# Two-block transformer on one Trainium2 core: the routing pipeline ahead of the experts, its instructions in another order

## The chip, the cores and the metric

The kernel runs on one core of one Trainium2 chip. The metric is the device time of one execution in microseconds, and the number given is the median of several runs. The core's engines are named as in the profile: PE is TensorE, DVE is VectorE, ACT is ScalarE, POOL is GpSimd, SP is SyncE, which here only issues transfers.

## What is computed

Two model blocks follow each other on an input of 512 rows by 1024. The first has two layers (pooling, retention and memory attention; then a sparse attention with memory attention). The second has a Fourier mix, a state-space mix and a mixture of experts. The change lies where the mixture of experts is prepared:

```python
x = x + merged @ w_out[i]
hn = _rmsnorm(x, ffn_norm_g[i])
x = x + _hier_moe(hn, router_group_w[i], ...)
...
x_pad = jnp.zeros((rows, d), h.dtype).at[dest].set(ht[tok_s])
a = jax.nn.silu(xb @ w_gate[e]) * (xb @ w_up[e])
return a @ w_down[e]
```

The router picks one of 8 groups for each row, and in it two of 8 experts, so 1,024 assignments go to 64 experts. Each expert has three float32 matrices (gate, up, down) of 1024 by 512 or 512 by 1024, 2,048 KB each, 192 in all. The output is the sum of each row's two weighted expert results, added to x and normalized.

## The kernel before

The program is a list of stages. The last two are `mix_out` and `moe`, and they share one block, with no barrier between them: each engine goes from its part of one to its part of the other when it gets there. Every engine's order is written out by hand, and engines meet at semaphores.

`mix_out` projects the merged mix (`project(n, m)`: column half n, row tile m of 4), adds it to `h` on DVE (`add`), normalizes each row tile (`norm` on DVE, the square sums and roots on ACT), turns h for the router (`turn` on PE, copies `take_hT` on DVE and line 2588 on ACT), computes the router's logits (`logits` on PE), chooses experts (`choose` on DVE), and ranks each row within its expert (`ranks` on PE, `rank` on DVE, which also makes the 0/1 matrix `picks0`). `hn` is split into a high and a low part: ACT rounds the high part (line 2590, semaphore `hn_high`), and POOL subtracts it from hn (line 2471, semaphore `hn_low`). `gather(m)` on PE multiplies both parts with `picks0` and so collects, in 4 PSUM banks, the rows of the first four experts. The banks are cleared beforehand by matmuls with zeros (line 2521). DVE copies the banks to `xT` (line 2681, semaphore `first_taken`), and counts per expert are made by PE (line 2568) and copied by DVE (line 2688).

`moe` then goes over 64 experts, e = 0 to 63. For each PE computes gate and up (`hidden`, line 2835, 64 instructions of weights and matmuls in two passes), gathers the rows of expert e + 4 (line 2815), turns the activated product, and after each pair of experts computes both results (`result`, line 2850). `place` (line 2827) makes row addresses once in 4 experts.

The 192 expert matrices are parts n = 0 to 191, six for each pair of experts: gate, up, gate, up, down, down. They land in 8 homes, part n in home n % 8. The first 8 are loaded by SP in `mix_out`. The homes of parts 5, 6 and 7 lie over memory that `mix_out` still uses: `h`, `hn`, and the block of `hT`, `picks0` and `zeros`. SP's queue waits for each in order:

```python
            sp.wait_ge(added, 2 * NT)
            sp.dma_start(k.x3_dram.rearrange("(m p) n -> p m n", p=P), h).then_inc(k.x3_stored, 16)
...
            sp.wait_ge(k.x3_stored, 16)
            load_expert_part(k, sp, 5)
            sp.wait_ge(hn_low, NT)
            load_expert_part(k, sp, 6)
            sp.wait_ge(lg_mm, NT)
            sp.wait_ge(gathered0, KD // 2)
            load_expert_part(k, sp, 7)
```

Parts 3 and 4 wait for `chunk_used`, the ends of the projection's two halves. In `moe` a part is loaded as soon as its home is free: part 8 when gate of expert 0 is done, part 9 when up of expert 0 is done, and so on, four of each six by SP and two (gate and up of one expert) by POOL after a pair's results.

Of the kernel before, what the change touches and what calls it, by code (L numbers as in the profile page):

```python
# [2348 lines left out]
def part_at(i, r):  # L2349

    return 6 * (i // 2) + (2 * (i % 2) + r if r < 2 else 4 + i % 2)
# [32 lines left out]
def mix_out(k):  # L2384
# [40 lines left out]
         "first_gathered", "first_taken"))  # L2425
    k.first_gathered, k.first_taken, k.counted = gathered0, taken0, c_mm
    first_banks = (0, 1, 6, 7)

    with k.block() as block:
# [35 lines left out]
        @block.gpsimd  # L2465
        def _(pool):
            pool.memset(ones, 1.0).then_inc(done, 1)
            pool.memset(k.zeros[0:1].bitcast(F32), 0.0).then_inc(zeros_set, 1)
            for m in range(NT):
                pool.wait_ge(hn_high, m + 1)  # L2470
                pool.tensor_tensor(k.hn_parts[:, 1, m, :, :], by_part[:, m, :, :],
                                   k.hn_parts[:, 0, m, :, :].bitcast(F32), ALU.subtract).then_inc(hn_low, 1)

        @block.tensor
        def _(pe):
# [8 lines left out]
            def turn(m):  # L2484
                pe.wait_ge(added, NT + m + 1)
                if m:
                    pe.wait_ge(hT_act, m)
                    pe.wait_ge(hT_dve, m)
                for j in range(2):
                    for kk in range(4):  # L2490
                        t = pe.transpose(k.ps[:, 2 + j, kk * P:(kk + 1) * P],  # L2491
                                         h[:, m, (4 * j + kk) * P:(4 * j + kk + 1) * P], k.ident)
                    t.then_inc(h_T, 1)
# [22 lines left out]

            def clear_first_banks():

                pe.wait_ge(zeros_set, 1)
                for b in first_banks:  # L2520
                    pe.matmul(k.ps[:, b, :], k.zeros[0:1, 0:P], k.zeros[0:1], start=True, stop=False)
# [30 lines left out]
            turn(2)  # L2552
            ranks(0)
            project(1, 3, range(KD // 2, KD))
            logits(2)
            turn(3)
            ranks(1)
            clear_first_banks()
            gather(0)
            logits(3)  # L2560
            ranks(2)
# [3 lines left out]
            gather(3)  # L2565
            pe.wait_ge(lg_in, NT)
            for m in range(NT):
                mm = pe.matmul(k.ps[:, 4, 0:NE], ones, M[:, m, :], start=m == 0, stop=m == NT - 1)
            mm.then_inc(c_mm, 1)

        @block.scalar
        def _(act):
# [4 lines left out]
            for m in range(NT):  # L2577
# [8 lines left out]
                if m >= 2:  # L2586
                    act.wait_ge(lg_mm, m - 1)
                act.copy(hT[:, m % 2, 4:8, :], k.ps[:, 3, :].rearrange("p (k s) -> p k s", k=4)).then_inc(hT_act, 1)
                act.wait_ge(gained, m + 1)
# [7 lines left out]
        def _(dve):  # L2597
# [17 lines left out]
            def norm(m):  # L2615
                dve.wait_ge(rooted, m + 1)
                k.link(dve, dve.reciprocal(rs[:, m:m + 1], sd[:, m:m + 1]))
                dve.scalar_tensor_tensor(out=hn[:, m, :], in0=h[:, m, :], scalar=rs[:, m:m + 1], in1=gain,
                                         op0=ALU.mult, op1=ALU.mult).then_inc(gained, 1)

            def choose(m):
# [39 lines left out]
            take_hT(0)  # L2661
            norm(0)
            add(1, 2)
            take_hT(1)
            choose(0)
            norm(1)
            norm(2)
            take_hT(2)
            choose(1)
            rank(0)  # L2670
            add(1, 3)
            take_hT(3)
            norm(3)
            choose(2)
            rank(1)
            rank(2)
            choose(3)
            rank(3)
            for piece in range(KD // 2):
                dve.wait_ge(gathered0, piece + 1)  # L2680
# [5 lines left out]
            k.link(dve, dve.tensor_reduce(sm[:, 4, :], eg, AX_X, ALU.add))  # L2686
            dve.wait_ge(c_mm, 1)
            k.link(dve, dve.tensor_copy(k.route.cnt, k.ps[:, 4, 0:NE]))

# [65 lines left out]
def moe(k):  # L2755

    nc, ps = k.nc, k.ps
    xT = k.xT
    t = k.misc
# [15 lines left out]
    with k.block() as block:  # L2775
# [27 lines left out]
        def _(pe):  # L2803
# [27 lines left out]
            def hidden(e, bank, w, done):  # L2831
                x = xT[:, e // FOUR % 2, :, SLOTS * (e % FOUR):SLOTS * (e % FOUR + 1)]
                for kk in range(KD):
                    for h in range(2):
                        mm = pe.matmul(ps[SLOTS * h:SLOTS * (h + 1), bank, 0:256], x[:, kk, :],  # L2835
                                       w[:, kk, 256 * h:256 * (h + 1)], start=kk == 0, stop=kk == KD - 1)
                mm.then_inc(done, 1)

            def result(pair):
                pe.wait_ge(aT_ready, 2 * pair + 2)  # L2840
                if pair:
# [13 lines left out]
            for e in range(NE):  # L2855
                if e < FOUR:
                    pe.wait_ge(k.first_taken, KD // 2)
                else:
                    pe.wait_ge(x_ready, 4 * (e // FOUR))
# [8 lines left out]
                wait_expert_part(k, pe, part_at(e, 1))  # L2868
                hidden(e, UP, expert_view(k, part_at(e, 1)), up_done)
                if e % FOUR == 0:  # L2870
                    place(e // FOUR)
# [31 lines left out]
        def _(dve):  # L2903
# [29 lines left out]
            for e in range(NE):  # L2933
                dve.wait_ge(silu_done, e + 1)
                dve.wait_ge(up_done, e + 1)
                if e >= 2:
                    dve.wait_ge(turned, e - 1)
                dve.tensor_tensor(a[:, e % 2, :], sg[:, e % 2, :], ps[:, UP, 0:256], ALU.mult).then_inc(a_ready, 1)  # L2938
                if e + FOUR < NE:
                    take(e + 4)  # L2940
# [340 lines left out]
```

## Time and profile before

| | us |
|---|---|
| median of 3 runs | 2478.43 (2476.04 to 2483.17) |
| profiled execution, its own time | 2479.41 |
| its span | 2477.6 |
| PE busy | 2250.2 (91%) |
| DVE busy | 793.8 (32%) |
| ACT busy | 471.3 (19%) |
| POOL busy | 251.4 (10%) |
| TensorE's granted clock, mean share | 0.967 |

The span is what the engines' records cover. The profiled execution took 1.8 us more than its span and 1.0 us more than the median. Busy shares are means over a dozen stages with different limits, so what a change in one stage is worth has to be read in that stage. `mix_out` runs from about 1406 to 1499 us of the span, `moe` from there to the end.

### The profile page before, as it was taken

The page shows a single profiled execution, that of the slowest core. Times are in us where ns is not written, and L with a number is a line of the kernel's source. Part 1 is how long each engine was busy: PE and PEld are TensorE (multiplying, and loading weights), DVE is VectorE, ACT ScalarE, POOL GpSimd, SP SyncE. Part 2 cuts the span into 40 slices and gives each one's busy share as a digit, 9 for nine tenths or more (in the row PEclk, how much of TensorE's full clock was granted, in tenths as well). Part 3 has the DMA queues.
Part 4 walks back from the last instruction along what each step waited for, and adds up shares of the span by engine and source line. Part 5 has one row for each costly group of instructions (what it writes and reads, how often), then busy time and mean ns, then how long its engine had stood idle before and what let it go on. Part 6 is the DMA issues. An engine that isn't in the chain of part 4 may idle for free. (4 is left out here: it accounts for less than half of the span.)

```text
span 2477.6 us, 32053 instructions
## 1 busy us (share of the span) xinstructions
PE 2250.2 (91%) x13664; PEld 1643.0 (66%) x13664; DVE 793.8 (32%) x1645; ACT 471.3 (19%) x834; POOL 251.4 (10%) x232
## 2 busy tenths in 40 slices
PE   8899978999999998899988999989998998889984
PEld 5788857888888677778874456555555555555552
DVE  6453246233322777444252242111111111111102
ACT  3222213131132544242211030000000000000001
POOL 0620000011000000650000010000000000000000
PEclk9999999999998999999999999999999999999997
DMA  7443212344331000435163449999999999999996
GB/s 220 154 136 119 69 46 86 109 160 145 97 119 34 10 22 14 171 128 174 56 122 120 148 173 383 426 425 425 426 425 425 424 425 423 421 421 426 424 420 241
DMA packets 130835, 569.16 MB, mean 230 GB/s; under 512 B 30563, under 2 KB 44503, under 8 KB 96855
## 3 DMA queue, kind: packets, MB, share of 16 engines
q1 hardware_dynamic: 110308, 409.47, 43.6%
q0 software_dynamic: 19232, 153.41, 15.3%
q10 hardware_dynamic: 1152, 4.19, 0.5%
q8 instruction: 111, 1.82, 0.3%
q14 instruction: 32, 0.26, 0.0%
HBM read 543.63 MB, written 35.80 MB: 234 GB/s over the span
## 5 line engine op out<-in xcount | busy, mean ns | idle before, releaser
L476 PE MATMUL ps<-w_parts,u_parts 128*128 128x512 f32 (+3 forms) x2016 | 426.2, 372 | 13.5 <-DVE u_parts L656 6.8
L476 PEld LDWEIGHTS ps<-w_parts,u_parts 128*128 128x128 f32 x2016 | 363.2, 189 | 71.7 <-DVE u_parts L656 8.0
L2835 PE MATMUL ps<-mem,mem_u 128*64 128x256 f32 x3072 | 348.3, 382 | 6.0 <-DVE mem_u L2919 3.8
L2835 PEld LDWEIGHTS ps<-mem,mem_u 128*64 128x64 f32 x3072 | 225.7, 137 | 118.8 <-issue 15.5
L443 DVE TENSOR_TENSOR w_parts<-w_raw,w_parts 128x2048 fp32r<-128x2048 f32 (+3 forms) x76 | 170.3, 2241 | 395.1 <-ACT w_parts L438 395.1
L2938 DVE TENSOR_TENSOR mem_c<-mem_c,ps 128x256 f32<-128x256 f32 x64 | 26.9, 421 | 712.7 <-issue 586.5
L2850 PE MATMUL ps<-mem,mem_c 128*64 128x512 f32 x768 | 191.5, 656 | 60.2 <-DMA mem<-in_expert_w_down 59.6
L438 ACT CAST w_parts<-w_raw 128x2048 fp32r<-128x2048 f32 (+3 forms) x76 | 134.9, 1776 | 486.0 <-PE ps L476 194.2
L2850 PEld LDWEIGHTS ps<-mem,mem_c 128*64 128x64 f32 x768 | 66.6, 150 | 174.1 <-issue 173.0
L474 PE MATMUL ps<-u_parts,w_parts 128*128 128x512 f32 x768 | 176.8, 390 | 0.0
L1442 PE MATMUL ps<-w_parts,u_parts 128*128 128x512 f32 x768 | 174.9, 390 | 0.0
L474 PEld LDWEIGHTS ps<-u_parts,w_parts 128*128 128x128 f32 x768 | 143.6, 188 | 31.2 <-issue 1.7
L1442 PEld LDWEIGHTS ps<-w_parts,u_parts 128*128 128x128 f32 x768 | 144.3, 188 | 29.9
L2896 ACT ACTIVATE mem_c<-ps 128x256 f32<-128x256 f32 x64 | 24.6, 385 | 571.9 <-PE ps L2835 571.9
L2815 PE MATMUL ps<-picks,hn_parts 128*128 128x256 f32 x960 | 130.6, 289 | 0.0
L2815 PEld LDWEIGHTS ps<-picks,hn_parts 128*128 128x128 f32 x960 | 118.4, 191 | 17.3 <-issue 17.3
L2835 PE MATMUL ps<-mem_u 128*64 128x256 f32 x1024 | 115.4, 381 | 4.1 <-DVE mem_u L2919 3.8
L2835 PEld LDWEIGHTS ps<-mem_u 128*64 128x64 f32 x1024 | 74.6, 137 | 41.7 <-DVE mem_u L2919 5.1
L2890 ACT COPY mem_u<-ps 128x512 f32<-128x512 f32 x64 | 34.4, 589 | 319.4 <-PE ps L2850 319.4
L1804 PEld LDWEIGHTS ps<-mem_u 128*128 128x128 f32 x480 | 59.0, 191 | 30.8 <-ACT mem_u L1859 24.2
L2365 POOL DMA_DIRECT2D mem<-in_expert_w_gate x23 | 12.9, 560 | 649.6 <-PE ps L2850 649.6
L1804 PE MATMUL ps<-mem_u 128*128 128x128 f32 x480 | 63.5, 279 | 16.2 <-ACT mem_u L1859 16.0
(390 smaller groups left out, 2359.3 us busy)
## 6 DMA issues: line engine op xcount, KB each, us to landing
mem<-in_expert_w_down SPq DMA_DIRECT2D x48, 2048.0 KB, 33.1
mem<-in_expert_w_gate SPq DMA_DIRECT2D x25, 2048.0 KB, 36.7
mem<-in_expert_w_up SPq DMA_DIRECT2D x25, 2048.0 KB, 27.7
mem<-in_expert_w_gate POOLq DMA_DIRECT2D x23, 2048.0 KB, 13.9
mem<-in_expert_w_up POOLq DMA_DIRECT2D x23, 2048.0 KB, 23.2
mem_u<-in_expert_w_down SPq DMA_DIRECT2D x16, 2048.0 KB, 34.6
w_raw<-in_od_w_in SPq DMA_DIRECT2D x18, 1024.0 KB, 5.0
mem_u<-in_expert_w_gate SPq DMA_DIRECT2D x9, 2048.0 KB, 36.7
```

Source lines behind the costliest of these rows:

```text
L438: act.copy(self.part(n, 0), self.raw(n)).then_inc(self.high, 1)
L443: dve.tensor_tensor(self.part(n, 1), self.raw(n), self.part(n, 0).bitcast(F32), ALU.subtract).then_inc(self.low, 1)
L474: mm = pe.matmul(out, w[x][:, kk, g.t * P:(g.t + 1) * P], u[:, y, ku, :], start=first, stop=last)
L476: mm = pe.matmul(out, u[:, x, ku, g.t * P:(g.t + 1) * P], w[y][:, kk, :], start=first, stop=last)
L1442: mm = pe.matmul(k.ps[:, g.bank, :], parts[g.part // 2][:, x, ky, g.t * P:(g.t + 1) * P], w[z][:, kk, :], start=g.part == 0 and kk == 0 an ...
L1804: mm = pe.matmul(o[:, 128 * i:128 * i + 128], pT[v % 2][:, 512 * i + kt * P:512 * i + kt * P + P], vv[:, kt, g * DH:(g + 1) * DH], start=k ...
L2815: mm = pe.matmul(o, k.hn_parts[:, part, m, 2 * r + j, :], k.picks[:, q % 2, m, :, :], start=m + part == 0, stop=m == NT - 1 and part == 1)
L2835: mm = pe.matmul(ps[SLOTS * h:SLOTS * (h + 1), bank, 0:256], x[:, kk, :], w[:, kk, 256 * h:256 * (h + 1)], start=kk == 0, stop=kk == KD - 1)
L2850: mm = pe.matmul(ps[SLOTS * i:SLOTS * (i + 1), ROWS + c, :], aT[:, i, j, SLOTS * h:SLOTS * (h + 1)], w[i][:, h, j, 512 * c:512 * (c + 1)], ...
L2890: act.copy(yn[:, pair % STORES, 512 * c:512 * (c + 1)], ps[:, ROWS + c, :]).then_inc(rows_ready, 1)
L2896: act.activation(sg[:, e % 2, :], ps[:, GATE, 0:256], ACT.Silu).then_inc(silu_done, 1)
L2938: dve.tensor_tensor(a[:, e % 2, :], sg[:, e % 2, :], ps[:, UP, 0:256], ALU.mult).then_inc(a_ready, 1)
```

## The change

No arithmetic is changed. (1) The subtraction that makes the low part goes from POOL to DVE, as `low(m)`; POOL has no compute in the stage after two memsets. (2) On DVE the last addition `add(1, 3)` still follows `rank(0)`, but norm(1) and norm(2), the low parts and the `take_hT` copies stand elsewhere; both last choices precede the ranks 2 and 3, and `low(3)` is last before the copies of the gathered banks. (3) On PE three banks are cleared inside the last projection, `ranks(1)` comes before `logits(2)`, and `logits(3)` comes ahead of `gather(0)`. For this the fourth turned tile uses bank 7 for its second half, and the gathers use bank 3 in place of 7. (4) In `moe` the gate of expert 0 waits for `first_taken` piece by piece, and the counts (four matmuls) and their copy stand behind the up of expert 0.

```diff
--- before.py
+++ after.py
@@ -2423,8 +2423,10 @@
...
          "first_gathered", "first_taken"))
-    k.first_gathered, k.first_taken, k.counted = gathered0, taken0, c_mm
-    first_banks = (0, 1, 6, 7)
+    k.first_taken, k.count_done = taken0, c_mm
+    k.ones, k.M = ones, M
+    first_banks = (0, 1, 6, 3)
+    turn_banks = [(2, 3)] * (NT - 1) + [(2, 7)]
 
...
@@ -2466,10 +2468,6 @@
...
             pool.memset(k.zeros[0:1].bitcast(F32), 0.0).then_inc(zeros_set, 1)
-            for m in range(NT):
-                pool.wait_ge(hn_high, m + 1)
-                pool.tensor_tensor(k.hn_parts[:, 1, m, :, :], by_part[:, m, :, :],
-                                   k.hn_parts[:, 0, m, :, :].bitcast(F32), ALU.subtract).then_inc(hn_low, 1)
 
...
@@ -2488,7 +2486,7 @@
...
                     for kk in range(4):
-                        t = pe.transpose(k.ps[:, 2 + j, kk * P:(kk + 1) * P],
+                        t = pe.transpose(k.ps[:, turn_banks[m][j], kk * P:(kk + 1) * P],
                                          h[:, m, (4 * j + kk) * P:(4 * j + kk + 1) * P], k.ident)
...
@@ -2514,10 +2512,9 @@
...
 
-            def clear_first_banks():
-
-                pe.wait_ge(zeros_set, 1)
-                for b in first_banks:
+            def clear(banks):
+
+                for b in banks:
                     pe.matmul(k.ps[:, b, :], k.zeros[0:1, 0:P], k.zeros[0:1], start=True, stop=False)
...
@@ -2551,22 +2548,20 @@
...
             ranks(0)
+            pe.wait_ge(zeros_set, 1)
+            clear(first_banks[0:3])
             project(1, 3, range(KD // 2, KD))
+            ranks(1)
             logits(2)
             turn(3)
-            ranks(1)
-            clear_first_banks()
+            clear(first_banks[3:4])
+            logits(3)
             gather(0)
-            logits(3)
             ranks(2)
...
             gather(3)
-            pe.wait_ge(lg_in, NT)
-            for m in range(NT):
-                mm = pe.matmul(k.ps[:, 4, 0:NE], ones, M[:, m, :], start=m == 0, stop=m == NT - 1)
-            mm.then_inc(c_mm, 1)
 
...
@@ -2585,7 +2580,8 @@
...
                     act.wait_ge(lg_mm, m - 1)
-                act.copy(hT[:, m % 2, 4:8, :], k.ps[:, 3, :].rearrange("p (k s) -> p k s", k=4)).then_inc(hT_act, 1)
+                act.copy(hT[:, m % 2, 4:8, :], k.ps[:, turn_banks[m][1], :].rearrange("p (k s) -> p k s", k=4)
+                         ).then_inc(hT_act, 1)
                 act.wait_ge(gained, m + 1)
...
@@ -2617,6 +2613,11 @@
...
                                          op0=ALU.mult, op1=ALU.mult).then_inc(gained, 1)
+
+            def low(m):
+                dve.wait_ge(hn_high, m + 1)
+                dve.tensor_tensor(k.hn_parts[:, 1, m, :, :], by_part[:, m, :, :],
+                                  k.hn_parts[:, 0, m, :, :].bitcast(F32), ALU.subtract).then_inc(hn_low, 1)
 
...
@@ -2660,22 +2661,26 @@
...
             norm(0)
+            norm(1)
+            low(0)
             add(1, 2)
+            choose(0)
             take_hT(1)
-            choose(0)
-            norm(1)
             norm(2)
+            low(1)
             take_hT(2)
...
             add(1, 3)
+            rank(1)
+            low(2)
             take_hT(3)
...
             choose(2)
-            rank(1)
+            choose(3)
             rank(2)
-            choose(3)
             rank(3)
+            low(3)
             for piece in range(KD // 2):
...
@@ -2684,8 +2689,6 @@
...
             k.link(dve, dve.tensor_reduce(sm[:, 4, :], eg, AX_X, ALU.add))
-            dve.wait_ge(c_mm, 1)
-            k.link(dve, dve.tensor_copy(k.route.cnt, k.ps[:, 4, 0:NE]))
 
...
@@ -2755,7 +2758,7 @@
...
     nc, ps = k.nc, k.ps
-    xT = k.xT
+    xT, count_out = k.xT, k.sem("moe_count_copied")
     t = k.misc
...
@@ -2831,12 +2834,22 @@
...
                 for kk in range(KD):
+                    if done is gate_done and e == 0:
+                        pe.wait_ge(k.first_taken, kk // 2 + 1)
                     for h in range(2):
...
 
+            def count():
+
+                for m in range(NT):
+                    mm = pe.matmul(ps[:, ROWS, 0:NE], k.ones, k.M[:, m, :], start=m == 0, stop=m == NT - 1)
+                mm.then_inc(k.count_done, 1)
+
             def result(pair):
+                if pair == 0:
+                    pe.wait_ge(count_out, 1)
                 pe.wait_ge(aT_ready, 2 * pair + 2)
...
@@ -2853,9 +2866,7 @@
...
             for e in range(NE):
-                if e < FOUR:
-                    pe.wait_ge(k.first_taken, KD // 2)
-                else:
+                if e >= FOUR:
                     pe.wait_ge(x_ready, 4 * (e // FOUR))
...
@@ -2867,6 +2878,8 @@
...
                 hidden(e, UP, expert_view(k, part_at(e, 1)), up_done)
+                if e == 0:
+                    count()
                 if e % FOUR == 0:
...
@@ -2936,6 +2949,9 @@
...
                 dve.tensor_tensor(a[:, e % 2, :], sg[:, e % 2, :], ps[:, UP, 0:256], ALU.mult).then_inc(a_ready, 1)
+                if e == 0:
+                    dve.wait_ge(k.count_done, 1)
+                    dve.tensor_copy(k.route.cnt, ps[:, ROWS, 0:NE]).then_inc(count_out, 1)
                 if e + FOUR < NE:
...
```

The order on PE at the end of `mix_out`, from the last half of the turned tile 1 to the first gathers. L2479 and L2477 are the projection, L2503 and L2501 logits, L2491 and L2489 turns, L2514 to L2515 and L2512 to L2513 ranks, L2521 and L2518 clears, L2529 and L2526 gathers. Before:

```order
L2491 MATMUL ps<-mem_c,mem 128x128 x8
L2515 MATMUL ps<-mem_u 128x64
L2479 MATMUL ps<-mem,mem_u 128x512 x4
L2503 MATMUL ps<-mem_u,mem 128x72 x8
L2491 MATMUL ps<-mem_c,mem 128x128 x8
L2514 MATMUL ps<-mem_u 128x64
L2515 MATMUL ps<-mem_u 128x64
L2521 MATMUL ps<-zeros 128x512 x4
L2529 MATMUL ps<-picks_55,hn_parts 128x256 x16
L2503 MATMUL ps<-mem_u,mem 128x72 x8
```

and now:

```order
L2489 MATMUL ps<-mem_c,mem 128x128 x8
L2513 MATMUL ps<-mem_u 128x64
L2518 MATMUL ps<-zeros 128x512 x3
L2477 MATMUL ps<-mem,mem_u 128x512 x4
L2512 MATMUL ps<-mem_u 128x64
L2513 MATMUL ps<-mem_u 128x64
L2501 MATMUL ps<-mem_u,mem 128x72 x8
L2489 MATMUL ps<-mem_c,mem 128x128 x8
L2518 MATMUL ps<-zeros 128x512
L2501 MATMUL ps<-mem_u,mem 128x72 x8
L2526 MATMUL ps<-picks_55,hn_parts 128x256 x16
```

Three of the four clears stand ahead of the projection's last piece, and all logits are computed before the first gather.

The order on DVE around the last addition (L2607, now L2603). L2642 and L2644, now L2643 and L2645, are a `rank`; L2619 is the new `low`; L2613, now L2609, is `take_hT`; L2617 and L2618, now L2613 and L2614, are a `norm`. Before:

```order
L2642 SCALAR_TENSOR_TENSOR mem_u<-ps,mem_u 128x64
L2644 TENSOR_TENSOR picks_55<-mem_u 128x256
L2607 TENSOR_TENSOR mem<-mem,ps 128x512
L2613 COPY mem<-ps 128x512
L2617 RECIPROCAL mem_c<-mem_c 128x1
L2618 SCALAR_TENSOR_TENSOR mem<-mem,mem_c,mem_u 128x1024
```

and now:

```order
L2643 SCALAR_TENSOR_TENSOR mem_u<-ps,mem_u 128x64
L2645 TENSOR_TENSOR picks_55<-mem_u 128x256
L2603 TENSOR_TENSOR mem<-mem,ps 128x512
L2643 SCALAR_TENSOR_TENSOR mem_u<-ps,mem_u 128x64
L2645 TENSOR_TENSOR picks_55<-mem_u 128x256
L2619 TENSOR_TENSOR hn_parts<-mem,hn_parts 128x1024
L2609 COPY mem<-ps 128x512
L2613 RECIPROCAL mem_c<-mem_c 128x1
L2614 SCALAR_TENSOR_TENSOR mem<-mem,mem_c,mem_u 128x1024
```

rank(1) and low(2) now stand between the last addition and the turned tile 3.

The order on PE where `moe` begins. L2568, now L2847, are the counts, L2835, now L2840, the gate and up of expert 0. Before:

```order
L2529 MATMUL ps<-picks_55,hn_parts 128x256 x32
L2568 MATMUL ps<-mem_u 128x64 x4
L2802 UNCONDITIONAL_BRANCH
L2835 MATMUL ps<-mem_u 64x256 x32
L2827 MATMUL ps<-slot_table,picks 128x2 x8
```

and now:

```order
L2526 MATMUL ps<-picks_55,hn_parts 128x256 x32
L2805 UNCONDITIONAL_BRANCH
L2840 MATMUL ps<-mem_u 64x256 x32
L2847 MATMUL ps<-mem_u 128x64 x4
L2830 MATMUL ps<-slot_table,picks 128x2 x8
```

The counts have moved behind the first 32 matmuls of `moe`.

## Rows read from the trace of the kernel before

**Rows 1.** The page: GB/s of the DMA engines in 40 slices of the span.

```profile
GB/s 220 154 136 119 69 46 86 109 160 145 97 119 34 10 22 14 171 128 174 56 122 120 148 173 383 426 425 425 426 425 425 424 425 423 421 421 426 424 420 241
```

**Rows 2.** Windows, core 0: from:to, length, busy of five engines, PEclk, DMA share, GB/s.

```profile
1474.00:1486.00 12.00, 8.26 (x39) 7.14 (x39) 10.24 (x26) 6.10 (x7) 4.14 (x2) 0.61 0.85 337
1486.00:1489.40 3.40, 3.40 (x29) 3.40 (x27) 1.94 (x1) 0.00 (x0) 1.65 (x1) 0.86 0.32 47
1489.40:1520.00 30.60, 29.03 (x251) 23.08 (x251) 13.05 (x36) 2.38 (x5) 0.00 (x0) 1.00 0.99 388
1520.00:1550.00 30.00, 29.46 (x226) 17.79 (x224) 4.02 (x7) 2.23 (x5) 2.17 (x3) 1.00 1.00 411
1550.00:2420.00 870.00, 786.56 (x5768) 492.30 (x5764) 103.39 (x230) 53.44 (x116) 60.76 (x87) 0.97 1.01 424
```

**Rows 3.** Who waited for whom, 1600 to 2450: us in total, times, longest.

```profile
PE ps L2850 <- DMA mem<-in_expert_w_down: 59.6, 19, 5.7
```

**Rows 4.** Timeline of SyncE's queue: start us, us, engine, line, operation.

```profile
1472.18 0.38 SPq L2365 DMA_DIRECT2D mem<-in_expert_w_down  x1
1479.27 0.38 SPq L2453 DMA_DIRECT2D x<-mem  x1
1487.60 0.37 SPq L2365 DMA_DIRECT2D mem<-in_expert_w_down  x1
1488.01 0.47 SPq L2365 DMA_DIRECT2D mem<-in_expert_w_gate  x1
1498.14 0.34 SPq L2365 DMA_DIRECT2D mem<-in_expert_w_up  x1
1502.90 0.33 SPq L2365 DMA_DIRECT2D mem_u<-in_expert_w_gate  x1
```

**Rows 5.** Line 2453 alone, the store of h: its time to landing.

```profile
DMA to landing us min/median/max: 8.2/8.2/8.2
```

**Rows 6.** Timeline of VectorE, ScalarE, GpSimd; [idle before <-releaser].

```profile
1466.54 2.08 ACT L2590 CAST hn_parts<-mem 128x1024 fp32r<-128x1024 f32 x1 [3.47 <-DVE mem L2618]
...
1470.23 2.41 DVE L2618 SCALAR_TENSOR_TENSOR mem<-mem,mem_c,mem_u 128x1024 f32<-128x1024 f32 x1
...
1474.80 2.85 POOL L2471 TENSOR_TENSOR hn_parts<-mem,hn_parts 128x1024 fp32r<-128x1024 f32 x1 [3.24 <-ACT hn_parts L2590]
...
1475.06 2.73 DVE L2599 TENSOR_TENSOR mem_c<-mem_u 128x128 f32<-128x128 f32 x1
...
1478.22 0.42 DVE L2644 TENSOR_TENSOR picks<-mem_u 128x256 fp32r<-128x256 f32 x1
1478.57 0.68 DVE L2607 TENSOR_TENSOR mem<-mem,ps 128x512 f32<-128x512 f32 x1
...
1481.25 1.29 DVE L2618 SCALAR_TENSOR_TENSOR mem<-mem,mem_c,mem_u 128x1024 f32<-128x1024 f32 x1
...
1482.45 0.28 DVE L2624 SCALAR_TENSOR_TENSOR mem_u<-ps,mem_c,mem_u 128x72 f32<-128x72 f32 x1
...
1485.07 2.87 DVE L2644 TENSOR_TENSOR picks<-mem_u 128x256 fp32r<-128x256 f32 x1
```

**Rows 7.** Part 5 of the page: busy us, mean ns | idle before, releaser.

```profile
L443 DVE TENSOR_TENSOR w_parts<-w_raw,w_parts 128x2048 fp32r<-128x2048 f32 (+3 forms) x76 | 170.3, 2241 | 395.1 <-ACT w_parts L438 395.1
```

**Rows 8.** Timeline of TensorE's matmuls.

```profile
1468.50 3.65 PE L2479 MATMUL ps<-mem,mem_u 128*128 128x512 f32 x8
...
1479.30 1.97 PE L2491 MATMUL ps<-mem_c,mem 128*128 128x128 f32 x8 [3.74 <-DVE mem L2607]
...
1481.94 2.07 PE L2521 MATMUL ps<-zeros 1*128 1x512 f32 x4
...
1493.97 4.08 PE L2529 MATMUL ps<-picks,hn_parts 128*128 128x256 f32 x32
1497.89 1.00 PE L2568 MATMUL ps<-mem_u 128*128 128x64 f32 x8
1499.18 7.13 PE L2835 MATMUL ps<-mem_u 128*64 128x256 f32 x64 [0.30 <-DVE mem_u L2681]
```

## The prediction

> **What bounds the kernel now.** I read the page's GB/s over the 40 slices first [rows 1]. Up to slice 24 (1486 us) the transfers move 10 to 230 GB/s, so other things bound; from slice 26 to the one before the last they stand at 421 to 426 and never dip. That is the expert weights. The windows say the same: 424 GB/s over 870 us at a DMA share of 1.01, while TensorE is busy for 787 of these 870 [rows 2]. Then the waits: after 1600 TensorE waits 59.6 us, 19 times, for down matrices in `mem` alone [rows 3]. So from about 1550 on, the stream of weights bounds the kernel, and TensorE, although 91% busy on the page, waits for it. The chain of waits ends in these transfers too, but it does not say where their delay begins. That must be sought where the stream last had holes: at 1486 to 1489.4 (47 GB/s), 1489.4 to 1520 (388) and 1520 to 1550 (411) [rows 2].
>
> So the changed stage matters in two ways. It starts TensorE's work on the experts earlier, which is a lead that TensorE later loses again while it waits for weights. And it starts weight transfers earlier, which is kept. The end moves by what the second is worth, unless the first is less.
>
> **The change on the engines: the last addition.** Before, `add(1, 3)` starts at 1478.57, although its matmuls, begun at 1468.50 and 3.65 long, ended near 1472.2 [rows 6, 8]. DVE was late, and three of its operations were long: a normalization of 2.41 us where another takes 1.29, a comparison in choose(1) of 2.73 beside neighbours of 0.2 to 0.4, and a `picks0` of 2.87 where another takes 0.42 [rows 6]. The second began at 1475.06 and ended at 1477.79; POOL's subtraction ran from 1474.80 to 1477.65 [rows 6]. The third is as long as a subtraction. The excess is 1.1 + 2.4 + 2.45 = 6 us. With POOL's four subtractions gone I take these three back to their short form.
>
> The Trainium skill's page SBUF — State Buffer, section "SBUF: two separate sides", says that VectorE operations with two SBUF inputs and a GpSimd operation that reads SBUF exclude one another for a whole instruction. The ends at 1477.79 and 1477.65 agree with it; by that rule too the excess goes and no new one comes.
>
> DVE pays four subtractions. Their nearest row is the same operation on twice the elements, mean 2.24 us [rows 7], so I take 1.15 each, 4.6 in all. Bounds: 0.7 (the 128x512 addition's 0.68 [rows 6]) and 2.85 (POOL's).
>
> norm(1) no longer stands behind choose(0), so ACT's rounding of tile 1 need not wait the 3.47 us that it did before 1466.54 [rows 6]. ACT is then done with the root of tile 2 some 3.3 us sooner, and norm(2), which started at 1470.23 with its reciprocal just ahead, can start near 1466.9. From there DVE does norm(2) 1.5, low(1) 1.2, a copy 0.7, choose(1) 2.4 (choose(2) ran from 1482.45 to just before 1485.07 [rows 6]) and rank(0) 0.7, which is 1473.4. The projection has three clears ahead of it now. Four took 2.07 at a granted clock of half [rows 2, 8], so three take 0.8 at full clock; with 0.2 for ranks(0), its last piece ends near 1473.2. DVE and PE meet, and the addition ends at 1474.1 in place of 1479.25: **5.1 us earlier**.
>
> **From there to the first expert.** PE: ranks(1) and logits(2) to 1475.8, turn(3) to 1476.8 (1.97 at half clock [rows 8], 1.0 at full). DVE: the copy to 1477.1, norm(3) to 1478.6, choose(2) to 1481.0; its first operation, done at 1478.9, releases logits(3), which ends at 1480.8. Then gather(0) 2.0 (two gathers take 4.08 [rows 8]) to 1482.8, ranks(2) 0.75 to 1483.6 (eight matmuls of this size take 1.00 [rows 8]), gather(1) to 1485.6, ranks(3) to 1486.6; DVE's rank(3) ends at 1487.4 and low(3) at 1488.6. gather(3) ends at 1490.8, and the gate of expert 0 follows at once, since its first piece of `xT` is copied while the gather still runs. Before it started at 1499.18 [rows 8]: **8.4 us earlier**. The counts cost nothing before, as they ran at 1497.89 while DVE copied the gathered banks; now their 1.00 us stands behind expert 0's up [rows 8]. TensorE's lead from then on is 8.4 - 1.0 = 7.4 us.
>
> **What the weight stream gets.** Here SP's queue counts, with every transfer that the addition lets go [rows 4]. Part 4 was issued at 1472.18 and h's store at 1479.27; it landed 8.2 us later [rows 5], and then part 5 went out at 1487.60, part 6 at 1488.01, part 7 at 1498.14, part 8 at 1502.90. Both the first two moved in 1474 to 1486, at 337 GB/s [rows 2]. Now part 4 goes out at 1473.3 (one us later, behind the clears) and the store at 1474.2. They overlap: 4.19 MB from 1475.1 on, at 396 (337 over the DMA share of 0.85) to 424 GB/s, take 9.9 to 10.6 us, say 10.2, to 1485.3. Before, nearly all of the 4.19 MB had moved near 1485.8 (337 GB/s over 12 us is 4.04 MB) and the store landed at 1479.27 + 8.2 = 1487.5, so I add 1.7 for the landing: 1487.0. Part 5 is issued at 1487.1. Of the addition's 5.1 us only **0.5** reaches the stream, because part 4 did not come forward. Bounds: 0 and 1.5 (if the store finishes ahead of part 4).
>
> The Trainium skill's page DMA: Bandwidth & Descriptors, section "Issuing engines are not separate DMA queues", speaks against a larger gain too: transfers of all queues share the same 16 DMA engines. By that rule the sum stays as it is.
>
> Then the holes. Part 5's first bytes flow 1.8 us after its issue (1487.60 to 1489.4, with 47 GB/s until then [rows 2]), at 1488.9, and a part of 2.10 MB takes 4.95 us at 424 GB/s. Part 6 is let go by low(3) at 1488.7, part 7 at 1490.9, part 8 at 1490.8 + 3.7 = 1494.5, the 3.7 being 1502.90 - 1499.18 of before [rows 4, 8]. At each of these times there are still 3 us or more of weights ahead, and the requests that follow come 7.4 us sooner than they did. So the stream stays at 424 from 1489 on. Before it lacked (424 - 388) x 30.6 = 1.10 MB up to 1520, which is **2.6 us**, and (424 - 411) x 30 = 0.39 MB up to 1550, **0.9 us** [rows 2]. The second is doubtful, since a dip can come from the transfers' own mix. The gain is 0.5 + 2.6 to 0.5 + 3.5, and I take 3.7: it is below TensorE's lead of 7.4, so the stream decides.
>
> The profiled execution took 2479.41, of which I expect 2475.7; against the median that is 2478.43 - 3.7 = **2474.7**.
>
> **The rivals.** (A) TensorE's lead counts in full: 7.4 us, 2471.0. For it: up to 1520 TensorE is busy in 29.03 of 30.6 us [rows 2] and so sets the pace there. Against it: the 424 GB/s over 870 us [rows 2] and the wait of 59.6 us [rows 3]. 2 in 10.
>
> (B) Slower. TensorE's granted clock is 0.5 of full (1.2 GHz, not 2.4) in matmuls that follow the idle 3.74 us before 1479.30 [rows 8], and 0.61 over 1474 to 1486 [rows 2]. In the new order it still idles from 1477.0 to 1479.0, where logits(3) waits for choose(2). If the clock falls there, logits(3), gather(0), ranks(2), gather(1) and ranks(3) take twice their 7.5 us; rank(3) and low(3) stand behind them, so low(3) ends at 1496.1 and gather(3) at 1498. Part 6 was issued at 1488.01 [rows 4]; it now is out at 1496, where the weights ahead ended at 1493.9. With the counts' 1.0 us on top, expert 0's up and all behind is level with before or late. That gives 2480. It decides from the point where low(3) ends later than about 1495.8, as each us after 1492.1 opens a hole of one us, and 3.7 use up the gain. Against it: before, shorter idle pieces such as the 0.30 ahead of 1499.18 left the clock alone, though none of 2 us is shown. 1 in 10.
>
> (C) The change does nothing for the end: part 5 still waits for the store and the holes stay as the transfers' own mix. 2478.4. 1 in 10.
>
> The forecast case has 6 in 10, and by its own bounds (a gain of 2 to 6, with the scatter of a median) lies between 2472 and 2477.
>
> **How the numbers follow.** The three runs before spread over 7 us, so I count 0.3%, 7.4 us, as what can be told from no change. A centre of 2474.7 is 3.7 below, hence same. Faster by more needs case A and a bit of luck, or scatter: 1 in 10 from A (its centre is just at the bound) and 1 in 10 from the forecast case. Slower by more needs B with more than its price: 6 in 100. The rest, 74 in 100, is same. The range reaches from 2470.0, past A, to 2480.5, past B.
>
> **What the changed kernel's profile would show.** DVE's operations of 2.4 to 2.9 us are gone, and its subtractions take 1.1 to 1.3 us; h's store is issued near 1474 and part 5 near 1487; part 6 waits for DVE's last subtraction near 1488.7; expert 0's gate starts near 1491 at full clock; GB/s from 1489 to 1550 is near 424. TensorE's waits for down matrices grow by some 4 us, its lead less the stream's. I am wrong if GB/s there stays near 400, if the end moves by the whole lead, or if the clock falls again before the gathers.

## The result, and the profile after

The changed kernel's median is 2472.43 us (22 runs), the kernel's before 2477.38 (22 runs). The ratio is 0.9982, 95% interval 0.9974 to 0.999: by the ratio 4.5 us or 0.18% faster, inside what I had called the same; the two medians alone are 4.95 us apart. The forecast was 3.7 us (2474.7, counted from the 2478.43 of three runs). The span of the profiled execution went from 2477.6 to 2472.3.

The windows of the changed kernel, from:to, length, busy time of PE, PEld, DVE, ACT and POOL, granted clock, DMA share, GB/s:

```profile
1474.00:1486.00 12.00, 10.08 (x63) 9.63 (x62) 8.88 (x29) 5.37 (x6) 0.00 (x0) 0.75 0.95 344
1486.00:1489.40 3.40, 3.40 (x28) 3.40 (x27) 0.65 (x2) 0.00 (x0) 0.00 (x0) 0.89 0.24 49
1489.40:1520.00 30.60, 29.82 (x255) 22.14 (x255) 12.27 (x24) 2.76 (x6) 0.00 (x0) 1.00 1.00 417
1520.00:1550.00 30.00, 29.46 (x216) 16.96 (x214) 4.02 (x7) 1.84 (x4) 2.16 (x3) 1.00 1.01 422
1550.00:2415.00 865.00, 784.58 (x5750) 491.45 (x5746) 103.43 (x230) 53.44 (x116) 60.79 (x87) 0.96 1.01 424
```

Against [rows 2]: from 1489.4 to 1520 417 GB/s flow in place of 388, from 1520 to 1550 422 in place of 411, and after that 424 in both. The first is worth (417 - 388) x 30.6 / 424 = 2.1 us, the second 0.8. Within the first the hole lay mostly in one stretch, before and then after the change:

```profile
1500.00:1510.00 10.00, 10.00 (x92) 7.42 (x90) 4.54 (x8) 1.27 (x2) 0.00 (x0) 1.00 0.94 362
```

```profile
1500.00:1510.00 10.00, 10.00 (x90) 7.74 (x88) 1.90 (x7) 0.39 (x1) 0.00 (x0) 1.00 1.00 429
```

It stood where parts 5 and 6 were nearly through and parts 7 and 8, which the gathers and the gate of expert 0 let go, had only just gone out. Now these go out 3.5 and 4.7 us sooner (rows below) and it is gone. This is read from the order of the rows; no run moves parts 7 and 8 alone.

TensorE's longest kind of wait for weights after 1600 is as it was [rows 3]; engine, line, waited for, us in total, times, longest:

```profile
PE ps L2863 <- DMA mem<-in_expert_w_down: 58.8, 20, 5.6
```

SyncE's queue, against [rows 4]: start us, us, operation.

```profile
1473.16 0.38 SPq L2365 DMA_DIRECT2D mem<-in_expert_w_down  x1
1474.06 0.38 SPq L2455 DMA_DIRECT2D x<-mem  x1
1487.73 0.37 SPq L2365 DMA_DIRECT2D mem<-in_expert_w_down  x1
1492.36 0.34 SPq L2365 DMA_DIRECT2D mem<-in_expert_w_gate  x1
1494.65 0.34 SPq L2365 DMA_DIRECT2D mem<-in_expert_w_up  x1
1498.21 0.33 SPq L2365 DMA_DIRECT2D mem_u<-in_expert_w_gate  x1
```

The store of h goes out at 1474.06, 5.2 us sooner, and part 5 at 1487.73, not sooner at all (1487.60). Part 6 is 4.4 us later than before, part 7 3.5 and part 8 4.7 us sooner. Two rows of TensorE's timeline and then VectorE's, against [rows 6, 8]:

```profile
1479.15 2.95 PE L2501 MATMUL ps<-mem_u,mem 128*128 128x72 f32 x16 [1.92 <-DVE mem_u L2625]
1481.85 3.76 PE L2526 MATMUL ps<-picks,hn_parts 128*128 128x256 f32 x16
...
1492.38 2.18 PE L2526 MATMUL ps<-picks,hn_parts 128*128 128x256 f32 x16 [0.78 <-DVE hn_parts L2619]
```

```profile
1472.29 0.29 DVE L2595 TENSOR_TENSOR mem_c<-mem_u 128x128 f32<-128x128 f32 x1
...
1473.35 0.68 DVE L2603 TENSOR_TENSOR mem<-mem,ps 128x512 f32<-128x512 f32 x1
...
1490.28 2.05 DVE L2619 TENSOR_TENSOR hn_parts<-mem,hn_parts 128x1024 fp32r<-128x1024 f32 x1
```

The last comparison of choose(1) takes 0.29 us, not 2.73, and the last addition starts at 1473.35, not 1478.57. But the new subtraction takes 2.05 us where I had 1.15, and logits(3) and gather(0) take 2.95 and 3.76 us (1.98 and some 2.0 at full clock), since the granted clock fell to half during logits(3), which starts after 1.92 us of idle time. gather(3), which waits for the last subtraction, starts at 1492.38, and the gate of expert 0 at 1494.49.

**Positions, not times of day.** The same code ahead of the stage ends at another time in each profile. This is the projection's first matmul in a kernel whose earlier stages are unchanged; before it stood at 1410.65, in the changed kernel at 1410.60:

```profile
1404.74 5.82 PE L2480 MATMUL ps<-mem,mem_u 128*128 128x512 f32 x13 [0.83 <-ACT mem_u L2572]
```

So below every position is counted from that matmul, in us. The columns "last but one in" and "last in" are the landings of the last two of the 192 matrices, both of them down matrices: the issue plus the time to landing. The expectations call the first of them "the last weights"; the stream ends with the second. The ratio is to the kernel before, run again beside each group of kernels (its median was between 2475.5 and 2477.4). One kernel stands in the table twice, as e_contig and e_contig_timed, and its two profiles differ by 1.4 us in the one column and by 0.8 in the other, so smaller differences there say little.

| kernel | its zero | part 5 out | part 6 out | gate 0 starts | last but one in | last in | ratio, 95% interval |
| --- | --- | --- | --- | --- | --- | --- | --- |
| before | 1410.65 | 77.0 | 77.4 | 88.5 | 1024.8 | 1030.8 | 1 |
| changed | 1410.60 | 77.1 | 81.8 | 83.9 | 1021.9 | 1027.0 | 0.9982 (0.9974 to 0.999) |
| e_moe_only | 1404.74 | 77.2 | 77.6 | 87.5 | 1024.5 | 1029.4 | 0.9994 (0.9984 to 1.0003) |
| e_pool | 1407.99 | 77.1 | 77.5 | 84.6 | 1021.6 | 1026.6 | 0.9994 (0.9985 to 1.0004) |
| e_contig | 1408.51 | 77.4 | 78.4 | 80.5 | 1021.9 | 1027.1 | not timed |
| e_contig_timed | 1409.98 | 76.8 | 78.4 | 80.5 | 1020.5 | 1026.3 | 0.999 (0.998 to 0.9999) |
| e_late5 | 1406.23 | 81.8 | 82.2 | 83.9 | 1025.8 | 1031.6 | 1.0002 (0.9993 to 1.0011) |
| e_warm | 1411.29 | 77.0 | 80.1 | 82.3 | 1020.8 | 1026.6 | 0.9991 (0.9982 to 1.0) |
| e_warm_low | 1408.37 | 76.9 | 77.3 | 81.3 | 1020.4 | 1026.6 | 0.9988 (0.9979 to 0.9997) |
| e_tiles | 1405.86 | 73.8 | 80.2 | 82.3 | 1020.0 | 1025.1 | 0.9986 (0.9977 to 0.9996) |
| e_all3 | 1406.04 | 73.5 | 76.0 | 82.9 | 1019.1 | 1025.0 | 0.9974 (0.9965 to 0.9983) |
| e_tiles_low | 1407.36 | 73.1 | 75.9 | 82.8 | 1018.9 | 1024.9 | 0.9974 (0.9964 to 0.9985) |
| e_best | 1410.31 | 68.2 | 75.7 | 81.3 | 1018.2 | 1023.1 | 0.9983 (0.9974 to 0.9992) |

### The profile page after: what moved, and what is told of

The parts are those of the page before. It is cut to its first block and busy times, and to the rows that moved or that the text cites. A ratio compares the mean times of both kernels' runs of the same rounds, so it can differ in the third digit from the quotient of the medians.

```text
span 2472.3 us, 32053 instructions
## 1 busy us (share of the span) xinstructions
PE 2250.2 (91%) x13664; PEld 1643.1 (66%) x13664; DVE 797.7 (32%) x1649; ACT 471.2 (19%) x834; POOL 240.0 (10%) x228
## 5 line engine op out<-in xcount | busy, mean ns | idle before, releaser
L2840 PE MATMUL ps<-mem,mem_u 128*64 128x256 f32 x3072 | 348.3, 382 | 5.9 <-DVE mem_u L2932 4.4
L2840 PEld LDWEIGHTS ps<-mem,mem_u 128*64 128x64 f32 x3072 | 225.8, 137 | 118.9 <-issue 15.8
L2863 PE MATMUL ps<-mem,mem_c 128*64 128x512 f32 x768 | 193.3, 661 | 58.8 <-DMA mem<-in_expert_w_down 58.8
L2840 PE MATMUL ps<-mem_u 128*64 128x256 f32 x1024 | 115.4, 381 | 3.8 <-DVE mem_u L2932 3.8
L2840 PEld LDWEIGHTS ps<-mem_u 128*64 128x64 f32 x1024 | 75.1, 137 | 41.0 <-DVE mem_u L2932 5.1
```

Of the source, the lines that this page charges most:

```text
L2863: mm = pe.matmul(ps[SLOTS * i:SLOTS * (i + 1), ROWS + c, :], aT[:, i, j, SLOTS * h:SLOTS * (h + 1)], w[i][:, h, j, 512 * c:512 * (c + 1)], ...
```

## Experiments

The open question is what the prediction chose between: does the weight stream set the end (theory S), or TensorE's lead, the start of expert 0's gate (theory L)? In the change itself both moved alike, 2.9 us (by the last matrix 3.8) in the stream and 4.6 - 1.0 = 3.6 in the lead, so the result alone can't tell.

**e_late5: the stream alone, delayed.**

```diff
-            load_expert_part(k, sp, 5)
             sp.wait_ge(hn_low, NT)
+            load_expert_part(k, sp, 5)
             load_expert_part(k, sp, 6)
```

> The changed kernel with part 5 held back until the last low part is done, so it goes out 81.7 us after the projection's first matmul and not at 77.1. TensorE needs part 5 only for the first result near 108 us, so its gate of expert 0 still starts near 83.9. Theory S (the stream of weights decides): the transfers stand still 4.6 us longer, so the last weights land some 4.6 us later than the changed kernel's 1021.9, less the 0.7 us that it had in small holes: 1025.8 to 1026.5, and the time is 2476 to 2477. Theory L (the lead decides): no change, 1021.9 and 2472.4.

SyncE's queue, then the first matmuls of expert 0's gate, then the landing of the last down matrix but one; in the last fence the last three loads of SyncE, of which the latest issued, at 2405.8, is the longest to land:

```profile
1488.03 0.37 SPq L2365 DMA_DIRECT2D mem<-in_expert_w_down  x1
1488.44 0.47 SPq L2365 DMA_DIRECT2D mem<-in_expert_w_gate  x1
...
1493.81 0.33 SPq L2365 DMA_DIRECT2D mem_u<-in_expert_w_gate  x1
```

```profile
1490.10 7.13 PE L2840 MATMUL ps<-mem_u 128*64 128x256 f32 x64
```

```profile
DMA to landing us min/median/max: 29.7/29.7/29.7
```

```profile
L2365 SPq DMA_DIRECT2D mem<-in_expert_w_down x2: 378/378/379, 2402.4 to 2405.8; - x2
DMA to landing us min/median/max: 29.6/29.7/32.0
```

The gate starts 83.9 us after the projection's first matmul (1490.10 - 1406.23), as in the changed kernel, and part 5 goes out 4.7 us later. Parts 7 and 8 go out as before it. The last matrix but one is in 3.9 us later, at 1025.8, the last 4.6 later, at 1031.6, and the ratio is 1.0002: the whole gain of the change is gone, and the two intervals don't meet. TensorE does not wait for part 5: from 1490.10 on it never idles for a transfer until 1537.22, 23 us after the first result. So a delay of 4.7 us in a transfer that nobody waited for cost some 5 us at the end. Theory S stands, L falls.

**e_contig and e_contig_timed: the lead alone, enlarged.** The low parts hold other numbers here, so the kernel computes something else; it serves for its times alone.

```diff
-                dve.tensor_tensor(k.hn_parts[:, 1, m, :, :], by_part[:, m, :, :],
+                dve.tensor_tensor(k.hn_parts[:, 1, m, :, :], hn[:, m, :].rearrange("p (k c) -> p k c", k=KD),
```

> The changed kernel with one difference: the subtraction reads hn in its own order and not with a stride of eight elements, so the low parts hold other numbers. It measures one term: 1.15 us for a subtraction if the stride is what makes it 2.05 us, and 2.05 if something else does. With 1.15 the last low part ends 0.9 us sooner or more.

> The changed kernel with the subtraction reading hn in its own order (the low parts hold other numbers), now timed. Its profile showed the gate of expert 0 at 80.5 us, 3.4 sooner than the changed kernel's 83.9, and the last weights at the same place. Theory S: the median is the changed kernel's, 2472.4. Theory L: 3.4 us sooner, 2469.0.

The subtraction in e_contig: ns min/median/max, then first and last start.

```profile
L2619 DVE TENSOR_TENSOR hn_parts<-mem,hn_parts x4: 1216/1217/1220, 1457.6 to 1485.6; 128x1024 fp32r<-128x1024 f32 x4
```

It takes 1.217 us; in the changed kernel the same row has a median of 2.038. So the stride of eight elements makes the difference. The gate starts 3.4 us sooner. In the first profile the last matrix but one is in at the same 1021.9 and the last 0.1 us later than in the changed kernel, in the second 1.4 and 0.7 sooner. The timed ratio of 0.999 is no better than the changed kernel's. A lead of 3.4 us more bought at most 1.4.

**e_warm and e_warm_low: the lead again, by the clock and by the order.** Eight matmuls of zeros are added onto the cleared bank while TensorE waits for choose(2); in the second kernel low(3) also moves up.

```diff
             clear(first_banks[3:4])
+            for _ in range(8):
+                pe.matmul(k.ps[:, first_banks[3], :], k.zeros[0:1, 0:P], k.zeros[0:1], start=False, stop=False)
...
             choose(3)
+            low(3)
             rank(2)
             rank(3)
-            low(3)
```

> The changed kernel, with eight more matmuls of zeros that accumulate into the cleared bank 3 while TensorE waits for the last choose(2) (its 1.92 us idle before 1479.15). Expected of both theories: the granted clock stays at full, so logits(3) takes 1.9 instead of 2.95 us, gather(0) 2.0 instead of 3.8, and the gate of expert 0 starts near 1491.2 in place of 1494.5. Theory S (the stream of weights decides the end): the changed kernel lacks only (424 - 417) x 30.6 + (424 - 422) x 30 = 0.27 MB up to 1550, so the end comes at most 0.7 us sooner, 2471.7 to 2472.4. Theory L (TensorE's lead decides, the end follows the gate of expert 0): 3.3 us sooner, 2469.1.

> As the last, and low(3) stands ahead of rank(2), where VectorE idled 2.2 us, and no longer behind rank(3). Both theories: part 6 is issued near 1485 but behind part 5, which still waits for the store of h to 1487.7; gather(3) no longer waits for low(3), and the gate of expert 0 starts near 1489.2, 5.3 us sooner than in the changed kernel. Theory S: part 5 and the stream behind it begin at 1489.5 as before, so the end comes at most 0.7 us sooner, 2471.7. Theory L: 5.3 us sooner, 2467.1.

TensorE in e_warm:

```profile
1477.74 1.99 PE L2559 MATMUL ps<-zeros 1*128 1x512 f32 x8
1479.81 2.64 PE L2501 MATMUL ps<-mem_u,mem 128*128 128x72 f32 x16
1482.20 3.10 PE L2526 MATMUL ps<-picks,hn_parts 128*128 128x256 f32 x16
```

The zeros fill the idle time, yet logits(3) and gather(0) take 2.64 and 3.10 us: the clock fell again, for a shorter while (0.72 over 1480 to 1486 makes 3.4 us at half). So it is not shown that the idle time alone lets it fall. The gate started 1.6 and 2.6 us sooner, not 3.3 and 5.3. The last matrix but one was in 1.1 and 1.5 us sooner and the last 0.4 in both, around the 0.7 of theory S and far from the lead's. Neither beats the changed kernel in time.

**e_tiles, e_all3, e_tiles_low, e_best: the stream advanced.** The store of h goes out in four pieces as its tiles are added up. e_all3 has this, the zeros and the early low(3); e_tiles_low leaves out the zeros; e_best is e_tiles_low with the last piece ahead of part 4's load.

```diff
-            sp.wait_ge(added, 2 * NT)
-            sp.dma_start(k.x3_dram.rearrange("(m p) n -> p m n", p=P), h).then_inc(k.x3_stored, 16)
+            def store(m):
+                sp.wait_ge(added, NT + m + 1)
+                sp.dma_start(k.x3_dram.rearrange("(m p) n -> p m n", p=P)[:, m, :], h[:, m, :]).then_inc(k.x3_stored, 16)
...
+            for m in range(NT - 1):
+                store(m)
...
+            store(NT - 1)
...
-            sp.wait_ge(k.x3_stored, 16)
+            sp.wait_ge(k.x3_stored, 16 * NT)
```

> The changed kernel with the store of h in four pieces, each as its row tile is added up, so that only the last 0.5 MB is left when the last addition is done. TensorE's work is untouched. Part 5 goes out near 1481 in place of 1487.7; part 6 still waits for low(3) to 1492.4. Theory S: the 2.10 MB of part 5 move ahead of 1487, but then the transfers stand still until part 6's first bytes at 1494.2, so of its 4.95 us some 4.7 are lost again; the end moves by less than 1 us: 2471.4 to 2472.4. Theory L: 0, 2472.4.

> All three edits together: the eight zero matmuls, low(3) ahead of rank(2), the store of h by tiles. Part 5 goes out near 1481, part 6 near 1485, so weights flow without a hole from 1483 on in place of 1489.5, and the gate of expert 0 starts near 1489.2. Theory S: the stream gains 6 us and TensorE's lead 5.3, so the smaller decides, with the 0.7 of before: about 5.3 us sooner than the changed kernel, 2467.1, and 4.6 sooner than the same kernel with the store in one piece. Theory L: 2467.1, but the same as with the store in one piece.

> The changed kernel with low(3) ahead of rank(2) and the store of h by tiles, without the zero matmuls. Part 5 goes out near 73.6, part 6 near 76, the gate of expert 0 starts near 81.9. Theory S: the last weights land near 1019, as with the zero matmuls, and the time is 2470. Theory L: the lead is 2 us more than the changed kernel's, 2470.4.

> The changed kernel with low(3) ahead of rank(2), the store of h by tiles, and the last tile's store ahead of part 4's load. Counted from the first matmul of the projection: the store's last piece lands near 67.5, part 5 goes out near 68.5 (when the last norm is done), part 6 near 76, part 7 near 81.5, the gate of expert 0 starts near 81.3. Theory S: weights that had moved by 86 us are about one part more than in the changed kernel, so the last weights are issued 3 to 4 us sooner than its 991.8, limited by holes ahead of parts 6 and 7: 2468.5. Theory L: the lead is 2.6 us more than the changed kernel's: 2469.8.

e_all3's gate starts 1.6 us later than e_warm_low's (its logits(3) and gather(0) take 2.96 and 3.76 us), and still its last two matrices are in 1.3 and 1.6 us sooner and its ratio is the better, though the intervals overlap: once more the stream and not the lead. The two best ratios belong to kernels in which part 5 and part 6 both come forward; e_tiles, with part 6 held by the last subtraction, stands at 0.9986. Between neighbours in the table the ratios do not always follow the weights, as intervals of about 0.2% let one expect: the changed kernel's 0.9982 stands beside e_warm_low's 0.9988. SyncE's queue in e_tiles_low:

```profile
1442.68 16.68 SPq L2452 DMA_DIRECT2D x<-mem  x3
1469.91 0.38 SPq L2365 DMA_DIRECT2D mem<-in_expert_w_down  x1
1470.80 0.32 SPq L2452 DMA_DIRECT2D x<-mem  x1
1480.44 0.38 SPq L2365 DMA_DIRECT2D mem<-in_expert_w_down  x1
1483.25 0.33 SPq L2365 DMA_DIRECT2D mem<-in_expert_w_gate  x1
```

The last piece of the store is short, and part 5 goes out 10.5 us after part 4's load, not 14.6 as in the changed kernel; part 6 follows at 1483.25.

The direction of theory S held, its sizes did not. Part 5 went out 3 us later than first expected of e_tiles and e_all3 (73.8 and 73.5, not 70.4), as the store's last piece still went out behind part 4's load. e_tiles was to gain less than 1 us of stream and had 1.9; e_all3 was to gain 5.3 and had 2.8, by the last matrix 2.0; e_best was to gain 3 to 4 and had 3.7 and 3.9, but its median is 2471.8 and not 2468.5.

e_tiles_low and e_all3 are the fastest, at 0.9974, 6.4 us below the kernel before and 2 below the changed one, whose interval overlaps theirs. e_best has its weights in soonest of all, 1018.2 and 1023.1, and the ratio 0.9983; its interval overlaps theirs, so whether it is slower stays open. So does how much of the last 1 to 2 us of stream reaches the time.

**e_moe_only and e_pool: parts of the change.** The first is the kernel before with part (4) of the change. The second is the changed kernel with the subtraction on GpSimd. Their core lines, one fence each:

```diff
-            for m in range(NT):
-                mm = pe.matmul(k.ps[:, 4, 0:NE], ones, M[:, m, :], start=m == 0, stop=m == NT - 1)
...
+                    if done is gate_done and e == 0:
+                        pe.wait_ge(k.first_taken, kk // 2 + 1)
...
+                if e == 0:
+                    count()
```

```diff
+            for m in range(NT):
+                pool.wait_ge(hn_high, m + 1)
+                pool.tensor_tensor(k.hn_parts[:, 1, m, :, :], by_part[:, m, :, :],
+                                   k.hn_parts[:, 0, m, :, :].bitcast(F32), ALU.subtract).then_inc(hn_low, 1)
...
-            low(0)
-            low(1)
-            low(2)
-            low(3)
```

> The kernel before with the fourth part of the change alone: the gate of expert 0 waits piece by piece, and the counts and their copy stand behind its up. Counted from the first matmul of the projection, the gate should start 1.2 us sooner than before (87.3 in place of 88.5 us), and from the counts on TensorE leads by 0.2. Theory S (the stream of weights decides): parts 8 and 9 go out 1.2 us sooner, the rest 0.2, so the last weights are issued 0.2 to 1 us sooner. Theory L (the lead decides): 0.2 us.

> The changed kernel with the subtraction back on GpSimd, all else in the new order. If the move to VectorE is what made the gain, VectorE's long operations come back beside GpSimd's subtractions of 2.85 us, the last addition is late again, and the gain is gone: 2477. If the order made it, VectorE saves its four subtractions of 2.05 us, pays perhaps 1.3 + 2.4 us for long operations, the last low part is done near 73.5 us after the projection's first matmul in place of 81.7, and the gate of expert 0 starts 1 to 2 us sooner than in the changed kernel; the last weights are issued within 0.7 us of the changed kernel's: 2472.

Part (4) alone moved the gate by 1.1 us, the last matrix but one by 0.3 and the last by 1.4. The timing (0.9984 to 1.0003) can't tell it from nothing. In e_pool VectorE's long operations are back. Each starts beside a subtraction of GpSimd's and ends after it, the normalizations 1.1 us after and the short comparison 0.1:

```profile
1454.31 2.85 POOL L2473 TENSOR_TENSOR hn_parts<-mem,hn_parts 128x1024 fp32r<-128x1024 f32 x1 [50.22 <-ACT hn_parts L2590]
...
1455.84 2.41 DVE L2618 SCALAR_TENSOR_TENSOR mem<-mem,mem_c,mem_u 128x1024 f32<-128x1024 f32 x1
...
1462.43 2.87 POOL L2473 TENSOR_TENSOR hn_parts<-mem,hn_parts 128x1024 fp32r<-128x1024 f32 x1 [5.26 <-ACT hn_parts L2590]
...
1463.96 2.42 DVE L2618 SCALAR_TENSOR_TENSOR mem<-mem,mem_c,mem_u 128x1024 f32<-128x1024 f32 x1
...
1468.56 2.85 POOL L2473 TENSOR_TENSOR hn_parts<-mem,hn_parts 128x1024 fp32r<-128x1024 f32 x1 [3.26 <-ACT hn_parts L2590]
...
1468.80 2.75 DVE L2599 TENSOR_TENSOR mem_c<-mem_u 128x128 f32<-128x128 f32 x1
```

They cost 1.1 + 1.1 + 2.45 us, less than the four strided subtractions, 8.2. The gate starts 0.7 us later than in the changed kernel, where 1 to 2 sooner was expected, and the weights are in at the same place (0.3 and 0.4 us sooner). So in the profiles the order makes the gain, and moving the subtraction adds next to nothing. The timed ratio, 0.9994, is worse than the changed kernel's, but the intervals overlap by 0.0005; that share stays open.

## Why the prediction was right

**The bound.** Right, and now shown from both sides: a delayed transfer cost its delay, an enlarged lead bought little. (A slip of reading: the lowest of the late slices is 420 GB/s, not 421.) TensorE's waits for down matrices in `mem` did not grow by the forecast 4 us; they went from 59.6 to 58.8, as the lead came out at 3.6 us and not at 7.4.

**The three long operations.** Right: 1.28, 0.29 and 0.42 us in place of 2.41, 2.73 and 2.87, and e_pool brings the long ones back. The rule of the Trainium skill's page SBUF — State Buffer, section "SBUF: two separate sides", that such a pair excludes one another for a whole instruction, agrees with all three pairs of rows above: 1.1 us, the time from GpSimd's end to VectorE's, is most of a normalization's own 1.28.

**VectorE's subtraction.** Mis-sized: 1.15 us forecast, 2.04 measured, within the bounds. The row that I took reads in order; this one reads hn with a stride of eight elements, and in e_contig, without the stride, it takes 1.22. That is 3.6 us for the four, and e_contig's gate starts 3.4 us sooner.

**The last addition.** 1473.35 against a forecast of 1473.4, 5.2 us earlier. In part this was luck: low(1) took 0.9 us more than its term, while norm(2) started 0.3 to 0.5 us sooner and the small operations took less.

**From there to expert 0.** Forecast 1490.8, measured 1494.5. What rival B describes took place: the clock fell after 1.92 us idle, and with the slower subtraction the last low part was done at 1492.3 and not 1488.6 (rank(3) 3.0 us late, the subtraction 0.8 more). It stopped short of the price of B, because the clock was back at full after some 7 us (0.75 over 12 us and 0.89 over 3.4 us make 6.0 + 0.7 us at half). The lead was 4.6 - 1.0 = 3.6 us and not 7.4.

**Part 5.** Forecast 0.5 us sooner, measured 0.1 later: the store, issued 0.9 us behind part 4, landed 13.6 us after its issue, where the forecast had 12.8.

**The holes.** Forecast 2.6 to 3.5 us, measured 2.1 + 0.8 = 2.9. Part 6 went out at 1492.36, just before part 5 was through, so its lateness cost little. With part 5's term at nothing the sum is 2.9 us and not 3.7, and so much sooner was the last matrix but one. The last was 3.8 sooner; that this is close to 3.7 proves nothing, as two profiles of one kernel differ by 0.8 in it.

**Behind the weights.** The profile's span is 5.3 us shorter. TensorE's second-to-last result, before and after:

```profile
2420.93 8.78 PE L2850 MATMUL ps<-mem_u,mem_c 128*64 128x512 f32 x32 [3.52 <-DMA mem_u<-in_expert_w_down]
```

```profile
2417.17 7.09 PE L2863 MATMUL ps<-mem_u,mem_c 128*64 128x512 f32 x32 [3.44 <-DMA mem_u<-in_expert_w_down]
```

It starts 3.8 us sooner, and that is the stream's share. From there to the end of the last result it took 29.1 us before and 27.6 after. Most of this difference lies in the row itself: the granted clock was 0.81 over it before and 1.00 after. By these runs that is chance and no gain of the change: e_contig and e_contig_timed, the same kernel, took 7.09 us (clock 1.00) and 9.82 (0.72) for it. In the thirteen profiles the time from the landing of the last matrix but one to the end of the last result is 12.1 to 12.5 us where both last results ran at full clock, and 14.0 to 15.8 where one did not. So the measured 4.5 us is in part stream, 2.9 to 3.8, and the rest is inside the interval of the ratio.

## What to carry to other kernels

Where a stream of transfers bounds the last stage, look for its last holes, and judge a change in the stage ahead by what it does to the issue of the first transfers, not by how much sooner the compute starts. Ask of each of those transfers what lets it go: here the gathers and the first gate let parts 7 and 8 go, where the gain shows, while a store that queued behind a load held part 5, and one subtraction at the end of an engine's list held part 6. And compare profiles of a long program from a fixed instruction of the stage, not from the start of the span, and look at the granted clock in what follows the stream before you credit a difference there.

## What was not expected of the hardware

A VectorE subtraction on 128x1024 took 2.04 us with one operand read at a stride of eight elements and 1.22 us without. Matmuls of zeros with one row, 1.99 us of them without a gap, did not keep the granted clock up in e_warm. Near the end it held at 1.00 after 3.44 us of idle time in the changed kernel and fell after 3.52 in the kernel before. And the stages ahead of the projection ended anywhere from 1404.7 to 1411.3 us in the thirteen profiles of the table, which alone is more than the effect measured here.
